# One operation of 1024 columns for the low part of a weight chunk, and one PE wait per chunk, in a streamed expert layer

## The reference, cut to what matters

```
q   = (xb @ w_q) ...                            # 8 heads, 2 halves of 128
s   = einsum('thpd,hpkd->thpk', q, subkeys)     # 128 keys per half
s1,i1 = top_k(s[:,:,0], 16); s2,i2 = top_k(s[:,:,1], 16)
sc,pos = top_k(s1[...,None] + s2[...,None,:], 16)       # over 256 sums
g   = softmax(sc)
act = gelu(einsum('thkd,td->thk', u[idx], xb))
out = einsum('thk,thkd->td', g * act, v[idx])
```

## Time and profile before

| | |
|---|---|
| median of 3 runs | 4241.19 us (4235.29 to 4241.3) |
| profiled execution, its own time | 4241.91 us |
| its span, first to last instruction | 4240.1 us |
| PE busy | 3895.7 us, 92%, 28190 matmuls |
| DVE busy | 2728.8 us, 64% |
| ACT busy | 1877.2 us, 44% |
| mean granted clock of PE | 0.951 of 2.4 GHz |
| DMA | 565 MB read, 134 GB/s over the span |

### The profile page before, as it was taken

How to read it: one execution, slowest core, us unless ns; L and a number is a source line. 1 busy time by engine, 2 the same in 40 slices (tenths; PEclk the granted TensorE clock), 3 DMA queues, 4 the chain that set the end, 5 groups by cost and what they waited for, 6 DMA issues and landing times. The chain is left out here.

```text
span 4240.1 us, 71450 instructions
## 1 busy us (share of the span) xinstructions
PE 3895.7 (92%) x28190; PEld 3557.4 (84%) x28190; DVE 2728.8 (64%) x5368; ACT 1877.2 (44%) x3679; POOL 0.2 (0%) x4
## 2 busy tenths in 40 slices
PE   7999749989999999999999999989759899978999
PEld 4884548779998799999997899978349899977999
DVE  2535563338876867787668766654565488677666
ACT  2242222235556644544446544434224455565443
POOL 0000000000000000000000000000000000000000
PEclk9999869999999999999999999989769999999999
DMA  4221202225554455555553455523005355523555
GB/s 170 70 70 62 95 0 90 92 96 181 181 182 135 135 167 183 182 180 183 183 183 125 140 182 183 168 83 107 0 1 182 129 182 181 183 70 95 182 183 163
DMA packets 142199, 568.39 MB, mean 134 GB/s; under 512 B 15808, under 2 KB 17344, under 8 KB 130240
## 3 DMA queue, kind: packets, MB, share of 16 engines
q1 hardware_dynamic: 142016, 566.14, 41.6%
HBM read 565.03 MB, written 1.05 MB: 134 GB/s over the span
## 5 line engine op out<-in xcount | busy, mean ns | idle before, releaser
L1054 ACT ACTIVATE high<-ring 128x512 fp32r<-128x512 f32 x1632 | 1028.8, 632 | 1191.6 <-PE ps L503 607.9
L1503 DVE TENSOR_TENSOR low<-ring,high 128x512 fp32r<-128x512 f32 x1632 | 1090.2, 689 | 432.7 <-ACT high L1054 416.6
L902 PE MATMUL ps<-wt,high 128*128 128x256 f32 x6144 | 1116.1, 284 | 8.2 <-DVE low L1503 8.2
L503 PE MATMUL ps<-h2hi,high 128*128 128x256 f32 x3456 | 984.2, 285 | 26.9 <-DVE low L1503 26.9
L503 PE MATMUL ps<-h2lo,high 128*128 128x256 f32 x3456 | 979.5, 283 | 0.0
L503 PE MATMUL ps<-h2hi,low 128*128 128x256 f32 x3456 | 979.5, 283 | 0.0
L902 PEld LDWEIGHTS ps<-wt,high 128*128 128x128 f32 x6144 | 962.0, 193 | 8.7 <-issue 5.7
L902 PE MATMUL ps<-wt,low 128*128 128x256 f32 x3072 | 871.4, 284 | 0.0
L503 PEld LDWEIGHTS ps<-h2hi,high 128*128 128x128 f32 x3456 | 665.2, 192 | 27.8 <-issue 12.7
L503 PEld LDWEIGHTS ps<-h2lo,high 128*128 128x128 f32 x3456 | 665.3, 193 | 0.0
L503 PEld LDWEIGHTS ps<-h2hi,low 128*128 128x128 f32 x3456 | 664.8, 192 | 0.0
(11 more groups left out here) (167 smaller groups left out, 3980.3 us busy)
## 6 DMA issues: line engine op xcount, KB each, us to landing
ring<-u_in SPq DMA_DIRECT2D x384, 512.0 KB, 3.5
ring<-v_in SPq DMA_DIRECT2D x384, 512.0 KB, 3.5
ring<-win_in SPq DMA_DIRECT2D x56, 1024.0 KB, 4.8
ring<-wmod_in SPq DMA_DIRECT2D x24, 1024.0 KB, 4.8
ring<-wq_in SPq DMA_DIRECT2D x48, 512.0 KB, 3.6
ring<-wmod_in SPq DMA_DIRECT2D x48, 512.0 KB, 3.6
ring<-wbr_in SPq DMA_DIRECT2D x16, 768.0 KB, 4.1
ring<-wout_in SPq DMA_DIRECT2D x8, 1024.0 KB, 4.8
```

Source lines behind the costliest of these rows:

```text
L503: return pe.matmul(o, l_, r, start=first, stop=last)
L902: i = pe.matmul(o, w[:, k, :], wt[:, v % 2, b, :], start=first and j % 2 == 0 and w is w_hi and b == 0, stop=False, skip_group_check=True)
L1054: return act.activation(o, i_, f, **kw_)
L1503: return dve.tensor_tensor(o, a, b, op)
```

## The change

The low part of a chunk is made by one DVE operation of 1024 columns. It waits until both halves of the high part are made, and adds one to `low_made`. PE waits once per chunk, ahead of the first half. High parts, `half_free`, the matmuls, their order, the buffers and the DMAs stay.

```diff
 def dots(n, q, low_at, read_at):
     pe.wait_ge(cnt.sem("u_read"), read_at)
     o = ps[4 + q % 2][:, 0:SEQ]
+    pe.wait_ge(cnt.sem("low_made"), low_at)
     for hf in range(2):
-        pe.wait_ge(cnt.sem("low_made"), low_at + hf)
         half = slice(hf * HALF, (hf + 1) * HALF)
...
 def sums(n, v, low_at, ready_at, first=False):
     pe.wait_ge(cnt.sem("w_ready"), ready_at)
+    pe.wait_ge(cnt.sem("low_made"), low_at)
     for hf in range(2):
-        pe.wait_ge(cnt.sem("low_made"), low_at + hf)
...
 # one_in, one_out, in_range, both_range, out_range: the awaited value
-    dots(n, q, 2 * HN[key] + 1, q + 1)
+    dots(n, q, HN[key] + 1, q + 1)
...
-            dots(n, q, it * 8 + (2 * HN["u", pp, c] + 1), it * 4 + (q + 1))
+            dots(n, q, it * 4 + (HN["u", pp, c] + 1), it * 4 + (q + 1))
...
 def lo(key):
     n = PN[key]
-    for hf in range(2):
-        dve.wait_ge(cnt.sem("high_made"), 2 * HN[key] + hf + 1)
-        half = slice(hf * HALF, (hf + 1) * HALF)
-        tt(low[:, n % 4, half], raw[:, n % 4, half], high[:, n % 2, half].bitcast(F32), ALU.subtract
-           ).then_inc(cnt.sem("low_made"), 1)
+    dve.wait_ge(cnt.sem("high_made"), 2 * HN[key] + 2)
+    tt(low[:, n % 4, :], raw[:, n % 4, :], high[:, n % 2, :].bitcast(F32), ALU.subtract
+       ).then_inc(cnt.sem("low_made"), 1)
```

More of the change, by code:

```diff
@@ L933, in one_in @@
                     n, q = PN[key], QN[key]
-                    dots(n, q, 2 * HN[key] + 1, q + 1)
+                    dots(n, q, HN[key] + 1, q + 1)
                 def one_out(key, first=False):
                     n, v = PN[key], VN[key]
-                    sums(n, v, 2 * HN[key] + 1, v + 1, first)
+                    sums(n, v, HN[key] + 1, v + 1, first)
                 def in_range(pp, c0, c1):
@@ L952, in both_range @@
                             n, v = PN["v", pp, c], VN["v", pp, c]
-                            sums(n, v, it * 8 + (2 * HN["v", pp, c] + 1), it * 2 + (v + 1))
+                            sums(n, v, it * 4 + (HN["v", pp, c] + 1), it * 2 + (v + 1))
                             n, q = PN["u", nxt, c], QN["u", nxt, c]
-                            dots(n, q, it * 8 + (2 * HN["u", nxt, c] + 1), it * 2 + (q + 1))
+                            dots(n, q, it * 4 + (HN["u", nxt, c] + 1), it * 2 + (q + 1))
                 def out_range(pp, c0, c1):
@@ L961, in out_range @@
                             n, v = PN["v", pp, c], VN["v", pp, c]
-                            sums(n, v, it * 8 + (2 * HN["v", pp, c] + 1), it * 4 + (v + 1))
+                            sums(n, v, it * 4 + (HN["v", pp, c] + 1), it * 4 + (v + 1))
                 def mod_half(pp, m):
```

## The result

The changed kernel took 4246.91 us (median of 20 runs, 4242.38 to 4254.9), the kernel before 4237.42 (median of 20 runs beside it): a ratio of 1.0025, 95% interval 1.0018 to 1.0032. One of the 20 runs of the kernel before took 7237.65 us and is left out of that ratio. By the medians (4246.91 and 4237.42) it is slower by 9.5 us, where the forecast had 8.8. The profiled execution took 4246.37, its span 4244.6, the mean granted clock 0.951 as before.

The account below looks back on a forecast made before the run. PE was taken as the bound (busy 92%), with nobody waiting for DVE inside stages. Starts 4.8, long steps 3.3 and clock 0.7 sum to +8.8 us, carried onto the median 4241.2: 4250.0 us, +0.21%, range 4242 to 4258.

Parts of the forecast that it names:

- Steady flow: About 800 of 816 chunks: nothing gained or lost, 2.88 us each; slack for low falls from over 2.5 to 0.65 us.
- rival (b): PE's queue: fewer instructions make it faster; at 30 ns a chunk 24.5 us gained less 8.8, 4225.5 us; chance 0.06.
- Part 1, the starts: At six stage starts PE stands waiting for low: three start 0.53 us later, three 1.05, together 4.8 us.
- Part 2, the long steps: Six lows behind the ranking's 2048-column addition come late for PE: four cost 0.33 us, two 0.99, together 3.3.
- The 16 steps with 0.05 left: Ranking steps of two maxima, searches and replacements in the interleaved pass: 0.05 us to spare, costed at nothing.
- the later high halves behind ACT's table loads: In six rankings and at each pass's first gelu: 0.26 to 0.59 us left, so no cost.
- Part 3, the clock: PE may fall to 1.2 GHz after the longer wait at 1456: one chance in two, 0.7 us; bounds -1.3 to +5.2.
- (a): Stage starts pay 4.8 us but long steps little, or one half-clock stretch less: 4246 to 4247 us; chance 0.34.
- (c): DVE's next operation starts 1.22 us behind the wide low's start, not 1.13: +11.2 us, 4252.4; chance 0.14.
- (d): The 0.65 us slack proves too small; 0.1 us over it, every chunk pays: 82 us, 4323; chance 0.02.

Follow-up runs that it names:

- the two delays: Changed kernel with a dummy DVE operation of 384 or 768 columns ahead of the wide low in 252 v-alone chunks; 4251.38 and 4273.78 us.
- starts_halved: Changed kernel, but the six chunks that open a stretch keep two DVE operations and two PE waits; 4238.67 us, ratio 1.0005.
- pe_once: Kernel before with only PE's half of the change: DVE keeps two low operations, PE waits once, for the second; 4243.76 us, ratio 1.0016.
- step_split: Changed kernel with the ranking's 2048-column addition made as two of 1024 columns with a low between them; 4241.82 us, ratio 1.0009.
- two_waits: Changed kernel in which PE waits ahead of each half for the same value, the second wait always met; 4247.5 us, ratio 1.0026.
- both_mended: Changed kernel with opening chunks in halves and the 2048-column addition in two; 810 of 816 chunks stay wide; 4236.3 us, ratio 1.0000.
- wide_delay6: Changed kernel with a dummy 768-column DVE operation ahead of the wide low in 252 v-alone chunks; 4273.78 us, ratio 1.0083.
- after_again: The changed kernel measured once more, unaltered, beside the kernel before; 4246.47 us, ratio 1.0023.
- halves_delay6: Kernel before with a dummy 768-column DVE operation ahead of the second low half; 4236.89 us, ratio 0.9999.
- early_starts: Kernel before with high and low of the opening chunks prepared sooner; 4236.36 us, ratio 1.0000.
- early_wide: Changed kernel with high and low of opening chunks prepared sooner and the 2048-column addition in two; 4234.9 us, ratio 0.9997.

## Why the prediction was right

**Steady flow**: right. Chunks of 2.88, low at S + 0.86, the next operation 1.14 behind a wide low (forecast 1.13). The slack is bracketed by the two delays (0.47 free, 0.86 not); it was put at 0.65 and is rather 0.74 in the stretches of v alone. Against rival (b) I had put what DVE is spared at 57 us; it is 92 of busy time (1090.2 to 998.0) and buys as little. Three of the stage ends that the prediction gives (1310, 2264, 3729) are off by 12 to 19 us: the last chunks there start at 1326.06, 2249.21 and 3744.12 in the trace of before. No sum uses them.

**Part 1, the starts**: forecast 3 x 0.53 + 3 x 1.05 = 4.8, measured 4.76, and starts_halved takes exactly these back. pe_once shows what they consist of.

**Part 2, the long steps**: forecast six waits and 3.3; six waits and 3.3 (0.79 + 1.86 + 0.67), at the steps named, and step_split removes all six. That the sum is met to the tenth is luck: low came 0.07 later than computed at the four steps in u alone, and PE started 1.28 and not 1.37 behind low at four of the six. The 16 steps with 0.05 left did not pay; the later high halves behind ACT's table loads neither.

**Part 3, the clock**: forecast one fall in two for pass (0, 1), 0.7 us. It did fall, at 1.47 to 1.49 us, in both profiles of the changed kernel and in the three of two_waits and the delays, whose code is the same up to there. I had read that three starts are followed by 1.2 GHz; it is five of six, as the passes of (0, 0) and (1, 1) begin at it, and these two moved by -0.40 and +1.08, which I had not counted. Measured 2.15 for a term of 0.7: the one mis-sized term of the sum. What I took as the condition, the length of the wait, does not decide it: pe_once, behind 2.81 us of wait, did not fall there, and starts_halved, behind 2.20, did.

**The sum**: 4.8 + 3.3 + 0.7 = 8.8 was forecast, 4.76 + 3.3 + 2.15 = 10.2 is in the traces, 9.5 in the medians. That the medians lie nearer the forecast than the traces do is no merit of it. The forecast of 4250.0 lies 3.1 over the measured 4246.91 because the median of before that it started from was one of three runs and lay 3.8 over that of 20 (4241.19, 4237.42).

**The rivals**: (a), only a part shows, is contradicted by the twelve waits, though its time (4246 to 4247) is the measured one, for the reason just given. (b) by two_waits and both_mended. (c) by the 1.14. (d) did not happen; its price was wrong by a factor of two (wide_delay6), so 0.1 us over the slack would have cost about 41 us and not 82.

The two parts don't simply add. Taken away singly they move the median by 7.8 and 4.7 us, 12.5, when the change as a whole is 9.9. The medians alone would let this pass as scatter, as each difference has an error of some 4 us, but the traces say the same, in us over the kernel before:

| | trace, behind the block | median |
|---|---|---|
| after, after_again | 10.1, 10.1 | 9.5, 9.9 |
| two_waits | 10.1 | 10.3 |
| pe_once | 4.7 | 7.2 |
| starts_halved | 1.0 | 2.1 |
| step_split | 6.6 | 5.2 |
| both_mended | 0.0 | -0.9 |
| halves_delay6 | 0.2 | -0.3 |
| early_starts | 0.5 | -0.8 |
| early_wide | -3.0 | -2.3 |

Taking the starts away gives 9.1 in the trace, the steps 3.5, 12.6 of 10.1. The waits do add up; what doesn't is the clock, which in starts_halved stayed up at two places where it falls in before and after alike. So the price of the starts is 4.8 in waits and something more in clock that no single row names. What is open is why the clock falls at one place and not at another behind the same wait.

## What to carry to other kernels

Joining two operations of an engine that nobody waits for saves nothing, and takes slack from whoever reads the first half: find the places where the reader stands (a stage's start) or where a long step stands ahead of it, count them, and price each by the longer operation (and the second input it now awaits). Where the slack is comfortable everywhere else, exempting those few places gives the old time back. Moving a start by half a microsecond also moves where PE's clock falls, and with stretches that cost 1.5 us each this can be as much as the waits themselves: count it as a range. Before work is moved into an engine's idle time, look at when its input lands: in a strict order, a waiting instruction holds all that is behind it.

## What the runs showed of the hardware

**The length of a wait does not by itself decide the clock behind it.** At the start of pass (0, 1), PE waited 2.21 us for low both in the kernel before (1456.46, then 1.00) and in early_starts. The latter:

```profile
1457.40 0.36 PE L503 MATMUL ps<-h2hi,high 128*128 128x256 f32 x1 [2.21 <-DVE low L1508]
```

```profile
1459.30:1461.30 2.00, 2.00 (x11) 2.00 (x11) 0.69 (x1) 0.63 (x1) 0.00 (x0) 0.50 0.01 4
```

The same wait, and half the clock behind it. Over all thirteen profiles, this start fell to the lower level in two of five behind 2.20 or 2.21 us, and in seven of eight behind 2.74 or 2.81 us. These are fewer cases than they seem: five of the eight are the changed kernel up to this place (two_waits with one met wait more per chunk), and agree. The first v chunk of (0, 1) shows it too: behind a wait of 2.51 us the clock fell in before, both_mended and halves_delay6, and not in starts_halved. So the wait's length is not enough to forecast the fall; that a longer one makes it likelier is suggested by these counts and not shown.

**Run times of one program come in groups.** The 20 runs of the changed kernel: twelve from 4242.4 to 4247.0, six from 4249.8 to 4252.0, two at 4254.9. The kernel before: sixteen from 4235.0 to 4238.6, three from 4241.2 to 4241.9. The groups are some 4 us apart, as wide as the whole of part 1, and a profile of unchanged stages moved by 5.67 us. The profiles tie the two together. Two of the thirteen were taken on a run of an upper group, before (4241.91) and early_starts (4242.02), and in these two alone the block ahead of the first pass comes at 887.6 or 888.0; in the other eleven it comes between 881.5 and 883.9. Ahead of the block PE is at the lower clock for 177.5 us in the two and for 164 to 167 in the eleven, and is busy 762.8 us in before and 754.4 in after for the same work. So the step between these groups lies ahead of the first expert pass and goes with the clock; what starts it was not isolated, and the groups of the changed kernel at 4250 and 4255 have no profile.
